# Scores in two matmuls, v turned in the values' banks, mLSTM's sums by adding transfers, and six low parts on GpSimd: one change to a tuned encoder layer

## Time and profile before

| | us |
|---|---|
| median of three runs | 1977.51 |
| lowest, highest | 1974.56, 1981.68 |
| profiled execution | 1973.24 |
| its span, first to last instruction | 1971.4 |
| TensorE busy | 1926.5 |
| VectorE busy | 1362.8 |
| ScalarE busy | 890.1 |
| GpSimd busy | 221.4 |

### The profile page before, as it was taken

The page is one execution under the profiler, slowest core; times in us unless marked ns, Lnnn a source line. Parts: engine busy times, 40 slices in busy tenths (PEclk is TensorE's granted clock), DMA queues, the critical chain, the costliest instruction groups (busy, mean ns, idle before and its releaser), DMA issues.

```text
span 1971.4 us, 26974 instructions
## 1 busy us (share of the span) xinstructions
PE 1926.5 (98%) x8993; PEld 1580.3 (80%) x8993; DVE 1362.8 (69%) x2800; ACT 890.1 (45%) x1446; POOL 221.4 (11%) x240
## 2 busy tenths in 40 slices
PE   8999999999999999999999999999999899999999
PEld 6888887788888888888887878787787677777787
DVE  7677868778768768867867565665665856567655
ACT  5554326335435435334453335546446564455222
POOL 0231000110010010010000111110110111111111
PEclk9999999999999999999999999999999999999999
DMA  6676544564464465466369864562655836447554
GB/s 212 219 266 222 196 140 150 134 149 135 120 165 123 116 165 147 111 159 150 111 214 356 217 157 90 130 176 49 172 120 128 271 76 193 113 110 216 98 118 106
DMA packets 160473, 310.37 MB, mean 157 GB/s; under 512 B 18096, under 2 KB 37184, under 8 KB 156624
## 3 DMA queue, kind: packets, MB, share of 16 engines
q1 hardware_dynamic: 129568, 247.82, 38.1%
q0 software_dynamic: 28608, 53.49, 17.8%
q10 hardware_dynamic: 2160, 7.34, 1.0%
HBM read 198.60 MB, written 118.37 MB: 161 GB/s over the span
## 4 chain that ended last, share of the span: by engine, by line
PE 89%; issue 3%; DVE 3%; DMA 3%; ACT 1%; SPq 0%; POOL 0%; DVEq 0%; ACTq 0%; POOLq 0%
PE ps L855 23%; PE ps L859 23%; PE ps L857 23%; PE ps L1054 3%; PE ps L1026 2%; PE ps L1040 2%; PE ps L997 1%; PE ps L953 1%; PE ps L962 1%; PE ps L956 1%; PE ps L1028 1%; PE ps L1056 1%; PE ps L1059 1%; PE ps L874 1%; PE ps L875 1%
## 5 line engine op out<-in xcount | busy, mean ns | idle before, releaser
L855 PE MATMUL ps<-t_hi,w_hi 128*128 128x512 f32 x2184 | 878.3, 402 | 25.5 <-issue 10.4
L859 PE MATMUL ps<-t_hi,w_lo 128*128 128x512 f32 x2184 | 854.5, 391 | 0.0
L857 PE MATMUL ps<-t_lo,w_hi 128*128 128x512 f32 x2184 | 853.7, 391 | 0.0
L855 PEld LDWEIGHTS ps<-t_hi,w_hi 128*128 128x128 f32 x2184 | 412.1, 189 | 119.1 <-issue 37.9
L859 PEld LDWEIGHTS ps<-t_hi,w_lo 128*128 128x128 f32 x2184 | 411.7, 188 | 88.0
L857 PEld LDWEIGHTS ps<-t_lo,w_hi 128*128 128x128 f32 x2184 | 412.6, 189 | 81.4
L1383 DVE TENSOR_TENSOR w_lo<-s_tmp,w_hi 128x512 fp32r<-128x512 f32 x312 | 221.1, 709 | 174.1 <-ACT w_hi L1091 163.8
L1091 ACT CAST w_hi<-s_tmp 128x512 fp32r<-128x512 f32 x312 | 193.0, 619 | 291.8 <-PE ps L859 276.7
L1383 DVE TENSOR_TENSOR w_lo<-w_raw,w_hi 128x512 fp32r<-128x512 f32 x234 | 165.0, 705 | 143.3 <-ACT w_hi L1091 137.3
L1091 ACT CAST w_hi<-w_raw 128x512 fp32r<-128x512 f32 x234 | 144.8, 619 | 224.5 <-PE ps L859 221.6
L434 POOL DMA_DIRECT2D fin_dram<-xt x32 | 28.0, 876 | 844.3 <-ACT xt L1110 823.7
(11 more groups left out here) (226 smaller groups left out, 2293.7 us busy)
## 6 DMA issues: line engine op xcount, KB each, us to landing
w_raw<-w_all_dram SPq DMA_DIRECT2D x320, 256.0 KB, 4.1
fin_dram<-xt SPq DMA_DIRECT2D x128, 256.0 KB, 4.4
fin_dram<-xt POOLq DMA_DIRECT2D x128, 256.0 KB, 4.8
arena<-fin_dram SPq DMA_DIRECT2D x64, 512.0 KB, 7.4
outT_dram<-xt POOLq DMA_DIRECT2D x60, 256.0 KB, 4.2
arena<-xT_dram SPq DMA_DIRECT2D x44, 256.0 KB, 6.0
arena<-xT_dram SPq DMA_DIRECT2D x16, 512.0 KB, 4.5
outT_dram<-xT_dram SPq DMA_DIRECT2D x16, 512.0 KB, 5.1
```

The source lines that it names most:

```text
L855: nc.tensor.matmul(ps[:, bank, :], hi, t_hi[:, n, k, :], start=new and k == 0, stop=False, skip_group_check=True)
L857: nc.tensor.matmul(ps[:, bank, :], hi, t_lo[:, n, k, :], start=False, stop=False, skip_group_check=True)
L859: mm = nc.tensor.matmul(ps[:, bank, :], lo, t_hi[:, n, k, :], start=False, stop=k == KP - 1, skip_group_check=True)
```

## The change

1. **Scores.** The normed keys are kept in a wider tile, each half as two pairs of classes with copies of the 16-column edges around them, so that the 64 edge keys and the 128 keys of one class lie side by side. ScalarE makes the six copies of a head at step 9 (two halves, three each); the product with the norms is split in two halves; the first scores wait for the copies (`a_ke`). Scores are a matmul of 512 and one of 192 columns. Where the class is odd the edge part lies behind, so the masks and the turned probabilities take it from there.
2. **v.** The value transposes write banks 6 and 7 in place of 2 and 3, the edge part the second half of bank 3. Its copy out (`edge_values`) stands first in VectorE's step 12. The turned probabilities wait for it alone, the values for all v.
3. **mLSTM's sums.** Stage 3 and 4 take y's sums with plus in place of minus (the evictions of those groups multiply by -1 where needed, `negated`). Copies from DRAM to DRAM on SyncE (steps 226, 236, 351) and adding transfers on GpSimd (steps 231, 343, 355) make them; three loads, four VectorE sums and four stores go.
4. **Low parts.** In exchanges 1, 3 and 4 two of seven low parts are made by GpSimd (`POOL_LOW`): n = 2 and 6, n = 2 and 5, n = 0 and 4, at the same steps.

```diff
+BUILD_SPLIT = {1: 0, 3: 2, 4: 1, 5: 3, 6: 4, 8: 6, 9: 5}
 Y_SPLIT = {3: {3: 0, 5: 1, 6: 2, 8: 3, 9: 4, 10: 5, 11: 6}, 4: {3: 0, 5: 1, 6: 2, 7: 3, 8: 4, 9: 5, 10: 6}}
-YM_AT = 321
+POOL_LOW = {1: (2, 6), 3: (2, 5), 4: (0, 4)}
+YM_STEPS = (226, 231, 236, 343, 351, 355)
...
+                    if i == 0:
+                        sp.dma_start(a_q, src.to_broadcast([P, SEQ])).then_inc(bc_in[i], 16)
+                    else:
+                        for half in range(2):
+                            sp.dma_start(half_keys(half), pairs(src[:, half * HALF:(half + 1) * HALF])
+                                         .to_broadcast([P, 2, 2 * P])).then_inc(bc_in[i], 16)
...
+                if u == YM_STEPS[0]:
+                    sp.wait_ge(m_out, 16 * 2)
+                    for n in (4, 3):
+                        sp.dma_start(ty_dram[0, SUMS.index(n)], y[:, 0:KP, HALF:]).then_inc(ym_out, 16)
+                if u == YM_STEPS[2]:
+                    sp.wait_ge(ym_added, 16)
+                    sp.dma_start(ty_dram[0, SUMS.index(1)], ty_dram[0, SUMS.index(4)]).then_inc(ym_out, 16)
+                if u == YM_STEPS[4]:
+                    sp.wait_ge(ym_added, 48)
+                    sp.dma_start(ty_dram[0, SUMS.index(5)], ty_dram[0, SUMS.index(1)]).then_inc(ym_out, 16)
...
                 for b in range(TB):
-                    t = nc.tensor.transpose(flat(2)[:, b * P:(b + 1) * P],
+                    t = nc.tensor.transpose(flat(6)[:, b * P:(b + 1) * P],
                                             v_at[:, b * P:(b + 1) * P], ident[:])
...
-                nc.tensor.matmul(ps[:, 4, :], q, a_k[:, h * HALF:(h + 1) * HALF], start=True, stop=True)
-                nc.tensor.matmul(ps[:, 5, 0:CLASSES * EDGE], q, k[:, 1 - h, :, edge:edge + EDGE], start=True, stop=True)
-                nc.tensor.matmul(ps[:, 5, CLASSES * EDGE:MASK_B], q, k[:, 1 - h, c, :], start=True, stop=True
-                                 ).then_inc(a_s, 1)
+                q, other = by_class(a_q)[:, h, c, :], (1 - h) * K_HALF + OTHER_AT[c]
+                nc.tensor.matmul(ps[:, 4, :], q, half_keys(h), start=True, stop=True)
+                nc.tensor.matmul(ps[:, 5, 0:MASK_B], q, a_k[:, other:other + MASK_B], start=True, stop=True).then_inc(a_s, 1)
...
                 if i == 0:
-                    pe.wait_ge(a_va, 4 * g + 4)
-                    pe.wait_ge(a_vd, 2 * g + 2)
-                else:
+                    pe.wait_ge(a_vd, 2 * g + 1)
+                if 8 * g + i > 0:
...
+                if at == 9:
+                    act.wait_ge(a_rope, 3 * h + 3)
+                    for half in range(2):
+                        edge = 0 if half == 1 else P - EDGE
+                        src = half_keys(half).rearrange("p q (r n) -> p q r n", r=2)[:, :, :, edge:edge + EDGE]
+                        for j in range(3):
+                            at_ = half * K_HALF + j * K_PAIR
+                            ins = nc.scalar.copy(a_k[:, at_:at_ + EDGES].rearrange("p (q r n) -> p q r n", q=2, r=2), src)
+                        ins.then_inc(a_ke, 1)
...
-                    nc.vector.tensor_tensor(x2, bank, x1, ALU.add).then_inc(ev_d, 1)
+                    if negated(g):
+                        nc.vector.scalar_tensor_tensor(x2, bank, -1.0, x1, ALU.mult, ALU.subtract).then_inc(ev_d, 1)
+                    else:
+                        nc.vector.tensor_tensor(x2, bank, x1, ALU.add).then_inc(ev_d, 1)
...
             def softmax_dve(h, at):
+                if at == 12:
+                    edge_values(h)
...
+            def add_ym(u):
+                y = y_dram[0:ATT_HEADS].rearrange("k p s -> p k s")
+                if u == YM_STEPS[1]:
+                    pool.wait_ge(m_out, 16 * 2)
+                    pool.wait_ge(ym_out, 32)
+                    pool.dma_start(ty_dram[0, SUMS.index(4)], y[:, 0:KP, 0:HALF], accum_op=ALU.add).then_inc(ym_added, 16)
+                if u == YM_STEPS[3]:
+                    pool.wait_ge(m_out, 16 * M_HEADS)
+                    pool.wait_ge(ym_out, 48)
+                    for n in (1, 3):
+                        pool.dma_start(ty_dram[0, SUMS.index(n)], y[:, KP:, HALF:], accum_op=ALU.add).then_inc(ym_added, 16)
+                if u == YM_STEPS[5]:
+                    pool.wait_ge(ym_out, 64)
+                    pool.dma_start(ty_dram[0, SUMS.index(5)], y[:, KP:, 0:HALF], accum_op=ALU.add).then_inc(ym_added, 16)
+
+            def low_part(b, off):
+                n = (BUILD_SPLIT if b == 1 else Y_SPLIT[b]).get(off)
+                if n in POOL_LOW[b]:
+                    pool.wait_ge(th_done[n], t_made(n, b))
+                    src = t_src[n] if b == 1 else t_lo[:, n].bitcast(F32)
+                    nc.gpsimd.tensor_tensor(t_lo[:, n], src, t_hi[:, n].bitcast(F32), ALU.subtract).then_inc(tl_done[n], 1)
+
             for u in range(FIRST, UNITS):
                 added(*divmod(u, PRODUCTS))
                 for h in range(ATT_HEADS):
                     turned_rows(h, u - A_START[h])
+                add_ym(u)
+                for b in (1, 3, 4):
+                    low_part(b, u - BUILD_AT[b])
```

More of the change, by code:

```diff
@@ L42 @@
 MASK_B = KEYS - 4 * P
+EDGES = CLASSES * EDGE
+K_PAIR = 2 * P + EDGES
+K_HALF = 2 * K_PAIR + EDGES
+OTHER_AT = [c // 2 * K_PAIR + c % 2 * (EDGES + P) for c in range(CLASSES)]
 PRODUCTS = 7
@@ L282, in in_blocks, with half_keys, pairs @@
             return row.rearrange("p (c r n) -> p c r n", r=CLASSES, n=RUN)
+        def half_keys(h):
+            at = h * K_HALF + EDGES
+            return a_k[:, at:at + 2 * K_PAIR].rearrange("p (q n) -> p q n", q=2)[:, :, 0:2 * P]
+        def pairs(row):
+            return row.rearrange("p (q n) -> p q n", q=2)
         def flat(b):
@@ L378, in build_program @@
         a_ve = sem("a_ve")
+        a_ke = sem("a_ke")
         a_va = sem("a_va")
@@ L1405, in evict @@
                         stored(dve, X3, g - 1)
-                    nc.vector.tensor_tensor(x3, bank, x1, ALU.add).then_inc(ev_d, 1)
+                    if negated(g):
+                        nc.vector.scalar_tensor_tensor(x3, bank, -1.0, x1, ALU.mult, ALU.subtract).then_inc(ev_d, 1)
+                    else:
+                        nc.vector.tensor_tensor(x3, bank, x1, ALU.add).then_inc(ev_d, 1)
                 if n == 4:
@@ L1503, in build @@
                     build_sums(off)
-                n = {1: 0, 3: 2, 4: 1, 5: 3, 6: 4, 8: 6, 9: 5}.get(off)
-                if n is not None and not (b == 2 and n in KEPT):
+                n = BUILD_SPLIT.get(off)
+                if n is not None and not (b == 2 and n in KEPT) and n not in POOL_LOW.get(b, ()):
                     t_low(b, n)
@@ L1764, in normed @@
             def normed(h, i):
-                raw, out, w = (raw_a, a_q, scaled_w) if i == 0 else (raw_b, a_k, vec[:, 1:2])
                 dve.wait_ge(turned[i], 16 * (h + 1))
-                dve.wait_ge(bc_in[i], 16 * (h + 1))
-                nc.vector.scalar_tensor_tensor(out, raw, w, out, ALU.mult, ALU.mult).then_inc(a_rope, 1)
+                dve.wait_ge(bc_in[i], 16 * (i + 1) * (h + 1))
+                if i == 0:
+                    nc.vector.scalar_tensor_tensor(a_q, raw_a, scaled_w, a_q, ALU.mult, ALU.mult).then_inc(a_rope, 1)
+                    return
+                for half in range(2):
+                    k = half_keys(half)
+                    nc.vector.scalar_tensor_tensor(k, pairs(raw_b[:, half * HALF:(half + 1) * HALF]), vec[:, 1:2], k,
+                                                   ALU.mult, ALU.mult).then_inc(a_rope, 1)
             def masked(g, i):
@@ L2072, in shape_constants @@
                     edges[:, c] = entry(4 * (e - query) + c - own)
-            tables.append(edges.reshape(P, EDGE * CLASSES))
-            tables.append(entry(4 * (place + (P if half == 0 else -P) - query)))
+            tables.append(edges.reshape(P, EDGES))
+            if own % 2 == 0:
+                tables.append(entry(4 * (place + (P if half == 0 else -P) - query)))
     table = np.concatenate(tables, axis=1).astype(np.float32)
```

137 lines of the change are left out of this document (56 added, 81 removed).

## The result

| | before | after |
|---|---|---|
| median, us | 1975.12 (20 runs) | 1979.82 (20 runs) |
| ratio of after to before | | 1.0024, 95% interval 1.0014 to 1.0034 |
| the profiled execution, us | 1973.24 (span 1971.4) | 1981.93 (span 1980.1) |

The kernel became slower by 0.24%, 4.7 us; the forecast was 4.1 us faster. The time lies inside the prediction's wide range (1962 to 1984 us) and within the 6 us that it called no change, but the sign is the other one, and the interval leaves out 1. The median of before was measured again beside it, 2.4 us under the one that the forecast started from; the ratio is what counts. The two profiled executions are 8.7 us apart, so one pair of them shows the places but not the sizes; for these I use the same stretch in several kernels.

A forecast was written before the change was run, and what follows sets the result against it. TensorE was taken as the bound, busy 1926.5 of 1971.4 us, the rest waits. Terms: -7.9 - 7.5 - 4.8 + 6.0 + 2.4 + 4.8 + 2.9 = -4.1 us, from 1977.5 to 1973.5 us; eight in ten from 1962 to 1984.

The forecast's parts named there:

- v turned in the values' banks: Step 12 of each head: probability transposes no longer wait for the copy of turned values; 7.5 us saved, bounds 5 to 7.5.
- Adding transfers: mLSTM's sums: the wait and half clock after three loads at step 321 go; 4.8 us saved.
- the prediction's last sign of being wrong: After step 226: a transfer that delays mLSTM's loads would show the forecast wrong; no size given.
- The second rival: Step 351: adding transfers hold up SyncE ahead of masks, raw tiles and weights; +15 in all, 1992 us; chance 0.08.
- The copied key edges: Step 9 of heads: first scores wait for ScalarE's copies, keys ready 1.55 us later; +6.0 us, bounds 3.5 to 12.
- Scores in two matmuls: Attention scores: one 192-column matmul replaces those of 64 and 128, 0.12 us x 64; 7.9 us saved.
- the fourth rival: Scores: the merged matmul gains nothing, as a bank may want its own start; +4, 1981 us; chance 0.05.
- Low parts on GpSimd: Exchanges 1, 3, 4: each 4.8 us GpSimd instruction holds VectorE's two-SBUF-input work; +2.4, +4.8 and +2.9 us.
- the first rival: Exchanges: GpSimd doesn't hold VectorE for long, so they cost 2.2 in place of 10.1; 1965.5 us; chance 0.27.
- Exchange 1: Low parts t_lo(2) and t_lo(6) on GpSimd hold VectorE's w_lo, delaying products 111 and 117; +2.4 us.
- Exchange 4: Low parts t_lo(0) and t_lo(4) on GpSimd delay products 505 and 509; +2.9 us, from +2.2 to +3.5.
- S(453): Start of product 453, exchange 3: late behind edge copies and GpSimd's t_lo(5), 1577.3 in place of 1572.13; 4.8 us net.

The follow-up runs named there:

- e8: Kernel before with only v's part: values turned in banks 6 and 7, edges in bank 3; ratio to before 0.9971.
- e9: Changed kernel with all low parts and mLSTM's sums on VectorE again, key copies still on ScalarE; ratio to before 0.9985.
- e1: Changed kernel with all low parts of the exchanges on VectorE again; 1973.5 us, ratio to before 0.9996.
- e2: Changed kernel with mLSTM's sums again by loads, VectorE sums and stores, no adding transfers; 1977.7 us, ratio to before 1.0013.
- e7: Changed kernel with low parts, key copies and mLSTM's sums all on VectorE; 1963.97 us, ratio to before 0.9945.
- e3: Changed kernel with the last adding transfers at steps 323, 331 and 335 in place of 343, 351 and 355; ratio to before 1.0067.
- e11: e6 with its two copies and four adding transfers moved to steps 372 to 398, in heads 0 and 1; ratio to before 0.9970.
- e6: Changed kernel with key copies and all low parts on VectorE, adding transfers kept; ratio to before 0.9974.
- e5: Changed kernel with the six key copies of a head on VectorE, GpSimd's low parts kept; ratio to before 1.0010.
- e10: Changed kernel with each GpSimd low part made by four instructions of 512 columns in place of one of 2048; ratio to before 1.0037.

## Why the prediction was wrong, point by point

Undone in steps, the change reads, in ratios times 1975 us: v's part -5.7 (e8), scores with ScalarE's copies +2.8 (e9), adding transfers +2.2 (e1 against e9), low parts +5.5 (after against e1); together +4.8. By the intervals of the ratios each step is known to a little over 3 us, so v's part and the low parts are clear of zero, and the two between them are not by these pairs alone. Forecast were -7.5, -1.9, -4.8 and +10.1.

*v turned in the values' banks* is right: mechanism, wait gone, -7.5 against -5.7 in an interval of 3.6 to 7.9.

*Adding transfers*: **this step failed.** It was put as "the adding transfers go through GpSimd's queue, whose own stores behind them have a group of products before their tile is wanted". The wait at 1040 did go: 28.7 us in place of 33.5. (Even this term was read from an execution with a long wait: the four other profiles with the sums on VectorE, e2, e7, e8 and e9, take 31.6 to 32.6 there, so the gain is 3 to 4 us and not 4.8.) But group 49's last store is wanted at once, by the first loads of head 0, and the copy on SyncE's queue and the adding transfers share the transfer engines with it. In head 0 this costs 4.2 us in the profile of after and 1.1 to 1.4 in the other five with the transfers there; at steps 225 to 240 up to 4 us, where mLSTM's loads are waited for, as the prediction's last sign of being wrong had it (e2 and e8, without them there, are 1.2 and 1.1 us long too, so part of it is the run's own scatter). e3 and e11 show that the price comes back in another place, and e6 against e7 that it is larger than the gain, by 5.7 us. The second rival had the right transfers and the wrong victim. That its 1111 fits the landing at 1110.87 is luck: it had them issued near 1097 and done in 12.6 us; GpSimd issued the first at 1090.74, and the two took 20.1 us. Its price per packet was not reached in engine time: q0 has 2112 packets more for 0.188 x 16 x 1980.1 - 0.178 x 16 x 1971.4 = 341 us, 0.16 us each. But from issue to landing the two took what it had reckoned for its limit of 0.3 us (19 us); only the early issue kept SyncE from waiting, by 0.9 us. What was left out is that packets wait for one another: a full set of engines makes every other transfer late, the short ones too. That "Bounds: -5 to the second rival's price" stood there is no excuse: the rival had been given 0.08.

*The copied key edges*: the second term that failed, in its size. Forecast was a delay of 1.55 us and 6.0 us in all. The delay is smaller, 2.59 - 1.36 = 1.23 us, since copies of 64 columns are 0.15 us apart and not 0.2; the waits are larger, 9.9 us in seven heads of after (5.9 to 9.9 in the seven profiles with the copies on ScalarE, 0.1 in before), and they bring the lower clock in heads 1 and 7. The hidden part was read from one execution, and in head 0 it lay on the early side: in the thirteen profiles k's rotary transfer lands there 12.96 to 16.18 us after product 362 began (14.51 in before, 16.18 in after). A slack of half a microsecond that hangs on a transfer with 3 us of scatter is none. (These are thirteen executions of thirteen kernels; how much of the spread is one kernel's own, no run here shows.) In head 7 the transfer lands 0.5 to 2.8 us later in every kernel with the merged scores (17.0 to 19.3 after product 481 began) than in before and e8 (16.5); why, I have not tried.

*Scores in two matmuls.* The short pair is 0.33 us to the next group (1504.25 to 1504.58), before 0.44:

```profile
1503.29 1.12 PE L1047 MATMUL ps<-arena 128*128 128x512 f32 x2 [0.29 <-DVE mins L1831]
1504.25 0.49 PE L1048 MATMUL ps<-arena 128*128 128x192 f32 x2
1504.58 0.49 PE L1058 MATMUL ps<-ident,arena 128*128 128x128 f32 x3
```

Over all 64 blocks the median is 0.324 us, before 0.443, which gives 64 x 0.12 = 7.6 us for a forecast of 7.9; the fourth rival is out. The gain is real once the copies are off ScalarE: e7 against e8 is -0.0026, 5.1 us.

*Low parts on GpSimd.* The hold lasts as long as GpSimd's instruction, as forecast, and the first rival is out. Exchange 1 costs 2.6 to 3.7 us (forecast 2.4). Exchange 4 (steps 500 to 512) takes 41.9 to 43.2 us in the five kernels with whole low parts on GpSimd and 38.1 to 39.8 in the seven without any, 3.4 us more in the mean (forecast 2.9). Exchange 3's S(453) was forecast at 1577.3 and came at 1577.13; 0.7 us of that is chance, since S(448) too was later by as much, where the forecast counted from its old time:

```profile
1577.13 0.77 PE L874 MATMUL ps<-t_hi,w_hi 128*128 128x512 f32 x1 [4.97 <-POOL t_lo L2080]
```

But the sum gave these 4.8 us to GpSimd, with 1.9 for the copies' order alone in the first rival. The whole is right, 39.8 us against 35.3 with neither cause. But either alone takes the whole or most of it (39.9 us, and 39.7 and 38.4): they lie side by side and not end to end, and so e1 gives back exchanges 1 and 4 alone, 5.5 us, and not 10.1. The term that was mis-sized is exchange 3's share of the low parts: 4.8 forecast, next to nothing measured while the copies stay on ScalarE.

So the sign turned on about 7 us in the sums of mLSTM and nearly 5 in the scores' part; v's part fell short by 1.8 more, and 4.6 overcounted in the low parts made up for some of it: 7.0 + 4.7 + 1.8 - 4.6 = 8.9 us from -4.1 to +4.8. That the miss was not larger is luck.

## What to carry to other kernels

A transfer has no price of its own on a queue with room: look at the busy share of all transfer engines in that stretch, and if it is near full, find the closest-awaited load or store beside it, on whatever queue. When a wait is added to an engine that works in order, its price is the idle time in front of it, with all that stands behind. Where two causes are both long enough to set the same wait, undoing one shows nothing; only the pair does. And a slack behind a transfer is read from several executions.

## What the runs showed of the hardware that was not expected

- The hold works both ways. In e5 GpSimd's low part begins at 1564.32, while VectorE goes from one instruction with two SBUF inputs to the next; it is 6.87 us long in place of 4.5, and VectorE's are not stretched until 1566.69. The same is seen in exchange 4 of after, 5.88 us. (The Trainium skill, "SBUF — State Buffer", section "Who interferes with whom", says that the shared ports are an exclusive lock and that the order of issue decides who blocks. These two agree. The hold of 5.49 us in after does not quite: there w_lo's record begins at 1554.17, 0.33 us ahead of GpSimd's 1554.50, and it is held all the same.)
- Two adding transfers of 1 MB between places in DRAM, issued one behind the other, landed 14.7 and 19.5 us after their issue, the third 13.6, against the 4.4 us by which the prediction put its second rival out; the plain copy of 1 MB took 10.0 us. Beside them the stores of 256 KB took 10.7 us (median of 11), before 4.7, and the weights 8.1, before 4.2. (The Trainium skill, "DMA: Bandwidth & Descriptors", section "Issuing engines are not separate DMA queues", says that transfers of all issuing engines run on the same 16 and interleave; the trace agrees with 101% busy.)
- GpSimd's four pieces of 512 columns (e10) took 5.5 to 8.7 us together with VectorE between them, and 5.0 the once that VectorE was held through all four; one instruction of 2048 columns, with VectorE held, 4.5 to 4.6.
- VectorE's six copies of 128x64 took 0.69 us together, ScalarE's 0.98.
